# Expert weights in 2 MB pairs, one per page turn, and the last down products with the activations standing

## The reference

```
xt = h.reshape(T, D)
top_val, top_idx = lax.top_k(xt @ router_w, 2)
gates = softmax(top_val)
y = sum over e of combine[:, e] * ((silu(xt @ w_gate[e]) * (xt @ w_up[e])) @ w_down[e])
```

## Time and profile before

| what | value |
|---|---|
| median of 3 runs | 1586.06 us (1580.23 to 1589.87) |
| the profiled execution | 1578.8 us |
| its span | 1577.0 us |
| TensorE busy | 1450.5 us, 92% |
| weight loads busy | 1260.1 us, 80% |
| VectorE, ScalarE, GpSimd busy | 16%, 11%, 9% |
| bytes moved | 433.47 MB, 275 GB/s over the span |
| TensorE's granted clock | 1.00 (2.4 GHz) in the rows |

### The profile page before, as it was taken

One profiled execution on the slowest core, in us unless ns is written; L12 is line 12 of the kernel. 1 busy time (PEld: TensorE's weight loads), 2 busy tenths in 40 slices (PEclk: granted clock), 3 DMA queues, 4 the chain that ended last, 5 costly groups with the idle time before them and its releaser, 6 DMA issues.

```text
span 1577.0 us, 54544 instructions
## 1 busy us (share of the span) xinstructions
PE 1450.5 (92%) x25973; PEld 1260.1 (80%) x25973; DVE 254.1 (16%) x490; ACT 177.1 (11%) x383; POOL 143.1 (9%) x167
## 2 busy tenths in 40 slices
PE   9999999999999999888888898998998898988887
PEld 8786587777687865888888888888888788988886
DVE  3433310000143435000010010010010010000102
ACT  4123220000131332100000000000000000000001
POOL 2243200000022532200000000000000000000000
PEclk9999999999999999999999999999999999999999
DMA  9213344444242245999999999999999999999992
GB/s 341 98 43 134 107 161 160 160 160 148 95 160 107 68 153 225 364 382 376 362 375 362 371 373 370 379 379 372 376 371 381 349 384 369 380 358 382 385 366 110
DMA packets 133612, 433.47 MB, mean 275 GB/s; under 512 B 9082, under 2 KB 33916, under 8 KB 119052
## 3 DMA queue, kind: packets, MB, share of 16 engines
q1 hardware_dynamic: 132384, 427.69, 72.1%
q0 software_dynamic: 672, 2.14, 0.5%
q10 hardware_dynamic: 332, 0.13, 0.0%
HBM read 428.89 MB, written 1.05 MB: 273 GB/s over the span
## 4 chain that ended last, share of the span: by engine, by line
PE 89%; issue 7%; DVE 2%; ACT 1%; POOL 1%; DMA 0%; ACTq 0%; DVEq 0%
PE ps L1135 33%; PE ps L1159 16%; PE ps L984 9%; PE ps L683 8%; PE ps L995 4%; PE ps L846 4%; PE ps L694 3%; PE ps L1192 2%; PE ps L803 1%; PE ps L1064 1%; PE ps L716 1%; PE ps L813 1%; PE ps L679 1%; PE ps L709 1%; PE ps L823 1%
## 5 line engine op out<-in xcount | busy, mean ns | idle before, releaser
L1159 PE MATMUL ps<-LT_sb,ring 128*64 128x80 f32 x5376 | 202.6, 233 | 31.6 <-issue 31.0
L1159 PEld LDWEIGHTS ps<-LT_sb,ring 128*64 128x64 f32 x5376 | 195.5, 137 | 38.2 <-issue 36.3
L1135 PE MATMUL ps<-AT_sb,ring 128*64 128x80 f32 x5376 | 200.4, 233 | 26.4 <-issue 26.2
L1135 PE MATMUL ps<-wpost,ring 128*64 128x80 f32 x5376 | 200.4, 233 | 22.7 <-issue 21.1
L1135 PEld LDWEIGHTS ps<-AT_sb,ring 128*64 128x64 f32 x5376 | 194.6, 138 | 31.7 <-issue 31.0
L1135 PEld LDWEIGHTS ps<-wpost,ring 128*64 128x64 f32 x5376 | 193.8, 139 | 28.5 <-issue 25.9
L984 PEld LDWEIGHTS ps<-hT_sb,ring 128*128 128x128 f32 x768 | 136.2, 191 | 24.4 <-issue 9.1
L984 PE MATMUL ps<-hT_sb,ring 128*128 128x256 f32 (+1 forms) x768 | 155.7, 362 | 0.0
L683 PE MATMUL ps<-hT_sb,ring 128*128 128x256 f32 x576 | 128.2, 380 | 0.0
L683 PEld LDWEIGHTS ps<-hT_sb,ring 128*128 128x128 f32 x576 | 108.3, 190 | 14.8 <-DVE late L1637 0.5
L1988 POOL TENSOR_SCALAR small<-small 128x1 f32<-128x1 f32 x16 | 3.6, 222 | 1191.6 <-ACT late L1515 923.1
(11 more groups left out here) (285 smaller groups left out, 1148.8 us busy)
## 6 DMA issues: line engine op xcount, KB each, us to landing
ring<-in_moe_w_gate SPq DMA_DIRECT2D x84, 1024.0 KB, 8.5
ring<-in_moe_w_up SPq DMA_DIRECT2D x84, 1024.0 KB, 8.4
ring<-in_moe_w_down SPq DMA_DIRECT2D x84, 1024.0 KB, 8.0
late<-in_moe_w_up SPq DMA_DIRECT2D x28, 1024.0 KB, 8.0
late<-in_moe_w_gate SPq DMA_DIRECT2D x28, 1024.0 KB, 7.8
late<-in_moe_w_down SPq DMA_DIRECT2D x28, 1024.0 KB, 8.1
ring<-in_ffn_w_gate SPq DMA_DIRECT2D x11, 1024.0 KB, 5.4
ring<-in_ffn_w_up SPq DMA_DIRECT2D x11, 1024.0 KB, 8.1
```

Of the source, the lines that this page charges most:

```text
L1135: ins = mm(o[lo:lo + P // 2, :], pairs[:, m % 2, lo:lo + P // 2], xgT[e % 2][:, k, :], start=(k == 0 and m % 4 == 0), stop=(k == KD - 1), ...
L1159: ins = mm(o[lo:lo + P // 2, :], d[:, i, m * P + lo:m * P + lo + P // 2], moe_hid[:, 2 * j + i, :], start=(first and m % 4 == 0), stop=las ...
```

## The change

**Pairs.** Two units that follow each other in the queue and are of one chunk and kind become a pair of 2 MB that one `dma_start` loads and one semaphore (`pair_landed`) reports. There are 168 pairs in eight places (`pair_of`); the order of the places over `ring` and `late` is new, and of the pairs that are loaded before the loop four (8 MB) now come before the signal of the last output projection and four after it, where it was 10 MB and 6 MB. TensorE waits for a landing at each even unit.

**Down products by token.** Chunk 3 of the down products leaves `m_down` for `m_down_by_token`: the activations stand (128 x 80) and 512 columns of the weights move. A unit is then 4 calls in place of 32. They add straight into banks 6 and 7, [slot, d], on top of what `y_transposes` has put there from chunks 0 to 2. So `yT_copy` comes after d2, `y_transposes` after u3 of the same expert (now as matmuls against the identity, 4 instructions each where a transpose had 2), and d3 of the expert before stays at its place between g0 and u0.

**Marks.** The page marks are picked as before, and call 4 of each block by token is a mark too. Pair i of the queue is issued at the first mark after the pair in its place was used, at most one pair at a mark (`mark_of`). Evaluated on its own lists the new function gives 172 marks, of which 167 are page turns; 160 pairs are issued from mark 2 to mark 165, none of them on the same mark as another; an expert after the first is 5373 instructions, 20.99 pages. In seven of the eight experts the block by token lies between g0 and u0 of the next; in the first four of these it stands in one page (but for half a call), in the other three the page turn falls 5, 8 and 11 instructions behind its beginning. One pair is issued in the page that holds the rest of it.

```diff
-TURN_MARKS = (8,)
-TURNS_AHEAD = 3
-UNIT_CALLS = 32
+TURN_MARK = 8
+MARKS_AHEAD = 3
+BY_TOKEN = 3
+TILE_CALLS = 32
+TOKEN_CALLS = 4
+TOKEN_MARKS = (TOKEN_CALLS,)
...
-            + [tiles("u", e, 0)] + once(e, e - 1, "y", 8, 2, 8)
+            + [tiles("u", e, 0)]
...
-            + [tiles("u", e, 2), tiles("g", e, 3), tiles("d", e, 2), tiles("u", e, 3)]
+            + [tiles("u", e, 2), tiles("g", e, 3), tiles("d", e, 2), tiles("u", e, 3)] + once(True, e, "y", 8, 4, 8)
...
                 has_signal = i % signal_every == signal_every - 1
-                if has_signal and signal_every == UNIT_CALLS:
-                    free_at.append(len(turns) + 1)
-                if at >= place(passed + len(turns)) and not has_signal:
-                    turns.add((owner, name, i))
-    last = used_at[ROUND_UNITS - 1] - TURNS_AHEAD
-    issues = ROUND_UNITS - N_UNIT
-    unit_turn = [max(free_at[i], 1 + i * (last - 1) // (issues - 1)) for i in range(issues)]
+                if has_signal and how in ("tile", "token"):
+                    free_at.append(len(marks) + 1)
+                turned = at >= pages * PAGE + TURN_MARK
+                if not has_signal and (turned or how == "token" and i in TOKEN_MARKS):
+                    marks.append((owner, name, i))
+                    pages += turned
+    mark_of = []
+    for i in range(N_PAIR, ROUND_UNITS // 2):
+        mark_of.append(max(free_at[2 * (i - N_PAIR) + 1], mark_of[-1] + 1 if mark_of else 1))
+        assert mark_of[-1] <= used_at[2 * i] - MARKS_AHEAD
...
+        def pair_of(n):
+
+            home, at = ((ring, 5), (ring, 0), (late, 0), (late, 1), (ring, 1), (ring, 2), (ring, 4), (ring, 3))[n % N_PAIR]
+            return home[:, at * PAIR:(at + 1) * PAIR]
...
             def first_free(n):
 
-                if n < 6:
-                    sp_.wait_ge(ring_used, FIRST_MOE - NSLOT + 1 + n // 3)
-                elif n == 6:
+                if n < 2:
+                    sp_.wait_ge(ring_used, FIRST_MOE - NSLOT + 1 + n)
+                elif n == 2:
...
-                elif n >= 10:
-                    sp_.wait_ge(ring_used, FIRST_MOE - 1 + (n - 10) // 3)
+                elif n >= 4:
+                    sp_.wait_ge(ring_used, FIRST_MOE - 1 + (n - 4) // 2)
...
-                        sp_.wait_ge(unit_used, n - N_UNIT + 1)
-                        sp_.wait_ge(page_turn, UNIT_TURN[n - N_UNIT])
+                        sp_.wait_ge(unit_used, unit + 2 - N_UNIT)
+                        sp_.wait_ge(page_turn, PAIR_MARK[n - N_PAIR])
...
-                        dst = unit_of(n)
-                        src = moe_down[0, e][lo:lo + 2 * P, :].rearrange("(p i) d -> p (i d)", p=P)
+                        dst = pair_of(n).rearrange("p (b x) -> p b x", b=2)
+                        src = moe_down[0, e][lo:lo + 4 * P, :].rearrange("(b p i) d -> p b (i d)", b=2, p=P)
...
                 for m in range(KD):
-                    ins = nc.tensor.transpose(bank(6 + m // 4)[0:SLOTS, m % 4 * P:(m % 4 + 1) * P], yT[:, m, :], ident)
+                    ins = mm(bank(6 + m // 4)[0:SLOTS, m % 4 * P:(m % 4 + 1) * P], yT[:, m, :], ident,
+                             start=(m % 4 == 0), stop=False, skip_group_check=True)
...
+            def m_down_by_token(r, e, c):
+
+                pe.wait_ge(mhid_ready, per_round(r, MOE_CH * e + c + 1, N_CHUNK))
...
+                    for i in range(2):
+                        for hf in range(2):
+                            ins = mm(bank(6 + hf)[0:SLOTS, :], moe_hid[:, 2 * j + i, :], d[:, i, half(hf)],
+                                     start=False, stop=(last and i == 1), skip_group_check=True)
+                            turned(ins, e, f"d{c}", call)
+                            call += 1
+                    ins.then_inc(unit_used, 1)
...
-                        m_down(r, e - 1, MOE_CH - 1)
+                        m_down_by_token(r, e - 1, MOE_CH - 1)
...
-                    if e:
-                        y_transposes(r, e - 1)
...
                     m_in(r, "u", e, 3)
-                m_down(r, N_EXP - 1, MOE_CH - 1)
-                y_transposes(r, N_EXP - 1)
+                    y_transposes(r, e)
+                m_down_by_token(r, N_EXP - 1, MOE_CH - 1)
```

More of the change, by code:

```diff
@@ L78 @@
 N_UNIT = N_OWN + 4
+N_PAIR = N_UNIT // 2
+PAIR = 2 * UNIT
 def unit_queue():
@@ L104, with unit_calls @@
 FIRST_IN_PAGE = 103
-TURN_MARKS = (8,)
-TURNS_AHEAD = 3
-UNIT_CALLS = 32
+TURN_MARK = 8
[4 more added lines that the diff above has]
+TOKEN_MARKS = (TOKEN_CALLS,)
 WAITS = {"g0": 5, "u0": 1, "g1": 2, "d0": 2, "u1": 1, "g2": 2, "gather": 2, "d1": 1, "u2": 1, "g3": 2, "d2": 1,
          "u3": 1, "d3": 1, "y": 2, "s0": 1}
+def unit_calls(kind, c):
+    return TOKEN_CALLS if kind == "d" and c >= BY_TOKEN else TILE_CALLS
 def pe_order(e):
     def tiles(kind, owner, c, part=None):
-        calls = UNIT_CALLS * (MOE_TILES[c] // 2)
+        each = unit_calls(kind, c)
+        calls = each * (MOE_TILES[c] // 2)
         first, n = (0, calls) if part is None else (part * calls // 2, calls // 2)
-        return owner, f"{kind}{c}", f"{kind}{c}" if not part else None, first, n, 4, UNIT_CALLS
+        how = "tile" if each == TILE_CALLS else "token"
+        return owner, f"{kind}{c}", f"{kind}{c}" if not part else None, first, n, 4, each, how
     def once(flag, owner, name, n, size, signal_every):
-        return [(owner, name, name, 0, n, size, signal_every)] if flag else []
+        return [(owner, name, name, 0, n, size, signal_every, name)] if flag else []
     def piece(i):
-        return [(e - 1, "s", f"s{i}", 2 * i, 2, 4, 4)] if e else []
+        return [(e - 1, "s", f"s{i}", 2 * i, 2, 4, 4, "s")] if e else []
     more = e < N_EXP - 1
     return ([tiles("g", e, 0)] + ([tiles("d", e - 1, MOE_CH - 1)] if e else once(True, 0, "oh", 2, 2, 2))
-            + [tiles("u", e, 0)] + once(e, e - 1, "y", 8, 2, 8)
+            + [tiles("u", e, 0)]
             + [tiles("g", e, 1, 0)] + piece(0) + [tiles("g", e, 1, 1)] + piece(1)
@@ L144, in page_turns @@
-    passed = sum(m < FIRST_IN_PAGE for m in TURN_MARKS)
+    at, marks, free_at, used_at = FIRST_IN_PAGE - WAITS["g0"], [], [], []
+    pages = 1
     for e in range(N_EXP):
-        for owner, name, waits, first, calls, size, signal_every in pe_order(e):
+        for owner, name, waits, first, calls, size, signal_every, how in pe_order(e):
             at += WAITS.get(waits, 0)
             for i in range(first, first + calls):
+                if how in ("tile", "token") and i % signal_every == 0:
+                    used_at.append(len(marks))
@@ L165 @@
+    mark_of = []
+    for i in range(N_PAIR, ROUND_UNITS // 2):
+        mark_of.append(max(free_at[2 * (i - N_PAIR) + 1], mark_of[-1] + 1 if mark_of else 1))
+        assert mark_of[-1] <= used_at[2 * i] - MARKS_AHEAD
+    return set(marks), mark_of
+PAGE_TURNS, PAIR_MARK = page_turns()
 assert ROUND_UNITS % N_UNIT == 0
@@ L362, in build @@
         ring_used = sem("ring_used")
-        unit_landed = [sem(f"unit_landed{i}") for i in range(N_UNIT)]
+        pair_landed = [sem(f"pair_landed{i}") for i in range(N_PAIR)]
         unit_used = sem("unit_used")
@@ L442, in gate_up_down @@
             return g, u, d
+        def pair_of(n):
+            home, at = ((ring, 5), (ring, 0), (late, 0), (late, 1), (ring, 1), (ring, 2), (ring, 4), (ring, 3))[n % N_PAIR]
+            return home[:, at * PAIR:(at + 1) * PAIR]
         def unit_of(n):
[L446 to L453, removed]
+            return pair_of(n // 2)[:, n % 2 * UNIT:(n % 2 + 1) * UNIT]
         def gate_ks(c, j):
@@ L584, in moe_loads @@
             def moe_loads(r, first):
-                for (kind, e, c, j), n in UNITS.items():
-                    if first and n < N_UNIT:
+                for (kind, e, c, j), unit in UNITS.items():
+                    if unit % 2:
+                        continue
+                    n = unit // 2
+                    if first and n < N_PAIR:
                         first_free(n)
                     elif first:
-                        sp_.wait_ge(unit_used, n - N_UNIT + 1)
-                        sp_.wait_ge(page_turn, UNIT_TURN[n - N_UNIT])
+                        sp_.wait_ge(unit_used, unit + 2 - N_UNIT)
+                        sp_.wait_ge(page_turn, PAIR_MARK[n - N_PAIR])
@@ L597, in moe_loads @@
+                        src = moe_down[0, e][lo:lo + 4 * P, :].rearrange("(b p i) d -> p b (i d)", b=2, p=P)
                     else:
                         f = slice(MOE_AT[c] * P, (MOE_AT[c] + MOE_TILES[c]) * P)
-                        ks = gate_ks(c, j)
-                        dst = gate_unit(n, c)
-                        src = (moe_gate if kind == "g" else moe_up)[0, e][ks.start * P:ks.stop * P, f]\
+                        first_k, last_k = gate_ks(c, j).start, gate_ks(c, j + 1).stop
@@ L602, in moe_loads @@
+                        dst = pair_of(n).rearrange("p (k f) -> p k f", f=MOE_TILES[c] * P)
```

(7 more changed lines are left out.)

41 lines of the change are left out of this document (19 added, 22 removed).

## The result

The kernel with pairs takes 1598.1 us (median of 10 runs, 1591.2 to 1604.1) where the kernel before takes 1583.8 beside it (10 runs, 1574.2 to 1589.9). The ratio is 1.0093, 95% interval 1.0074 to 1.0112. The forecast was 16.5 us more and 1603 us; 14.2 us more and 1598 us were measured.

The account below looks back on a forecast made before the run. The experts were taken as bound by weight transfers, behind which instruction pages wait. Terms of 761.7, 141.2 and 38.2 us made 941.1 against 925.4; with start +2.5 and end -1.7, +16.5 us, median 1603 us, range 1572 to 1620.

Parts of the forecast that it names:

- The loop of weights and instruction pages: In the experts: the instruction page waits behind queued weights, so a page lasts as long as its two transfers, 5.48 us.
- Ordinary pages (1): In the experts: 139 page intervals with one pair each, bound by DMA at 5.48 us, 761.7 us in all.
- The block and what follows (2, 3): Seven pages with the block by token at 10.8 us, the next two 4.5 and 5.3 us; 141.2 us in all.
- First and last pages (4): The page from mark 1 to 2 and the pages after the last pair with the final block: 38.2 us.
- The sign "about 368 GB/s": Sign that the forecast is right: the transfer rate over the stage of the experts is about 368 GB/s.
- y (5): Transposes of y as matmuls after u3: nothing added in the middle, 1.7 us less at the end.
- The start (6): Start of the experts: 8 MB instead of 6 behind the signal delay it by 0 to 5.5 us, taken as 2.5.
- SP (7): SP's queue: 168 issues in place of 336 and the later landing of pairs change nothing.
- A: Rival on the experts' transfers: one of 2 MB runs better than two of 1 MB; faster, median 1561 us; chance 0.15.
- C: Rival on ordinary pages: queued 2 MB transfers hold instruction pages longer, 5.60 us a page, 1620 us; chance 0.10.
- B: Rival on the long pages: they are paid back, so no change; 1585 us, or 1596 counting rests alone; chance 0.28.

Follow-up runs that it names:

- e5: The changed kernel, but from the ninth pair on only the first half of each pair is loaded; one execution, 1477.6 us, 6.8% under the kernel before.
- e6: The changed kernel with calls by token one to a page over eight pages, seven pair places, 6 MB at the start, scatter moved; 1582.3 us, ratio 0.9988 to before.
- e1: The changed kernel with each pair loaded by two transfers of 1 MB at the same mark; 1596.6 us, ratio 1.0084 to the kernel before.
- e4: The kernel before with pairs of 2 MB in eight places, all down products still in tiles; 1590.8 us, ratio 1.0037 to the kernel before.

## Why the prediction was right

**The number.** The forecast was +16.5 us, and the medians are 14.2 us apart (12 to 18 by the interval). Part of this closeness is luck. Over the stage of the experts 18.2 us more were forecast, with the start, and 12.8 are in the traces; the 5.4 us too many were partly made up by things that I had not forecast, 1.7 us of a lower clock ahead of mark 1, and 1.5 us because the profiled executions stand 5.0 and 6.5 us under the medians of their kernels. By my own line, 1%, the outcome is "no change", to which I had given 0.38, against 0.47 for "slower".

**What bounds the kernel.** The loop of weights and instruction pages, a reading of two turns before, holds: e5 takes half the bytes away and 85 us of stops go with them, and the instruction packets of the traces time it.

**Ordinary pages (1).** The term was 5.48 us. Over 128 ordinary pages of the trace after the mean is 5.48 us (three more, just ahead of the blocks that a page turn cuts, last 4.43 at a DMA share of 1.01; why no stop ends them is open). In number I was off by one: the last pair goes at mark 165 with six page turns behind it, where I had five, so one page fewer is ordinary and one more stands at the end.

**The block and what follows (2, 3).** Forecast 10.8, 4.5 and 5.3 us; measured 11.25, 4.43 and 5.48. The block itself is 7.02 us (6.9 forecast). The DMA share over it is 0.72 where I expected near 0.8. Where the block is cut by a page turn the two pages are 8.5 and 6.9 us.

**First and last pages (4).** Forecast from the last pair on 33.8 us, measured 37.94: the page that I had counted elsewhere. From mark 1 to the last pair the forecast was 4.4 + 761.7 + 141.2 + 2.5 for the start = 909.8 us, and 900.28 were measured. 5.5 of the 9.5 us are that same page and 1.3 the start. The other 2.7 lie at the blocks: those three pages of 4.43 us, for which 5.48 were put, are 3.2 us less, and the rest of the blocks is 0.6 more. Over the whole stage 943.6 us were forecast with the start, and 938.2 measured. The sign "about 368 GB/s" did not fit the sum: the 366 GB/s of the stage before, over 941.1 us in place of 925.4, are 360, and 363 were measured.

**y (5).** Nothing was forecast in the middle and nothing shows; at the end -1.7 us forecast, -1.7 measured. **The start (6).** Forecast 2.5 us; the page from mark 1 to 2 is the place:

```profile
637.87:643.49 5.62, 4.66 (x134) 4.49 (x132) 0.00 (x0) 2.64 (x3) 5.62 (x3) 1.00 0.99 411
```

It is 5.62 us where 4.43 were taken before, so 1.2. With 6 MB behind the signal again, in e6, it is 4.43. The further 1.7 us before mark 1 are there at the first transfer of the experts already, 550.61 us against 548.94, and go with the clock. All nine traces agree: mark 1 falls at 636.2 us with no stretch at the lower level ahead of it, at 637.9 with one, at 639.7 to 640.2 with two, and at 640.6 to 641.5 with three.

**SP (7).** Nothing: e1 doubles the issues and the time stays.

**The rivals.** A (2 MB run better) falls by e1 and e4. C (2 MB hold instructions longer) falls by e1 and by the 5.48 us. B has something in it: the rests of the turns with one transfer before are indeed paid back, 6.4 us up to the last pair. But the end, where no transfer covers the pages and the block, takes twice as long as before, and the sum of B left that out. The time fell between B's 1596 and the forecast's 1603.

**What decides it.** Seven page turns fewer were worth nothing by themselves: 160 pairs at 5.48 us are 877 us in either kernel. What counts is the time in which the engines for the transfers rest. Up to the last pair the change moves that rest from the turns with one transfer to the seven long pages, and at the end it leaves 19 us more of it.

## What to carry to other kernels

Where a count of bytes sets the pace, as here, fewer instructions, pages or transfers were worth nothing by themselves; add up instead the stretches in which the bytes rest. A long piece of engine work that is cheap in sum is dear in one piece: cut it so that each part fits in the slack that the transfers leave in one interval (here 1.06 us), and price a part as it runs alone, not as it runs in the block. And look at what stands behind the last transfer: that work has no cover, and here it takes back what the better schedule gives (16.0 of 18.7 us in e6).

## What the runs showed that I had not expected

- Two matmuls of 512 float32 columns between others of 80 columns take 1.01 to 1.02 us; in a block of sixteen it is 0.88 for two (7.02 us). The eight lone calls of an expert cost 1.1 us more than the block.
- Halving the bytes took the stops of TensorE from 87 us to 1.6, with the DMA engines still busy for 62% of the stage. When a page of instructions arrives is not a matter of the mean load; it hangs on the queue that it finds.
- 2 MB last 5.48 us as one transfer or as two, 382 GB/s, and single windows of a page reach 404 to 411.
